# Taking the products of constants out of a decoder step's norm pauses, beginning and routing

## The chip, the cores and the metric

The kernel is one launch on one core of one Trainium2 chip. The metric is device time in microseconds, the median of the runs shown. The engines are named as in the profile: PE (TensorE; PEld is its weight load), DVE (VectorE), ACT (ScalarE), POOL (GpSimd), SP (SyncE, which here issues the weight DMAs).

## What is computed

Two layers of a decoder are run for 256 prompt tokens and 64 sample tokens (8 sequences of 8), 320 columns in all, model width 1024, all in fp32. Cut to what matters:

```
mod = (silu(c) @ w_ada[l] + b_ada[l])           # six vectors: sh1, sc1, g1, sh2, sc2, g2
h   = rmsnorm(x, norm_pre_mix[l]) * (1 + sc1) + sh1
mix = mixer(h)                                  # gMLP chunk gating and HGRN2, merged by w_out
x   = x + g1 * rmsnorm(mix, norm_post_mix[l])   # } a norm pause: post-norm, residual,
h   = rmsnorm(x, norm_pre_ffn[l]) * (1 + sc2) + sh2   # } pre-norm
f   = swiglu(h)        (layer 0: dense, 2816 wide)
f   = moe(h)           (layer 1: top 2 of 8 experts by h @ w_router, 2816 wide each)
x   = x + g2 * rmsnorm(f, norm_post_ffn[l])
```

No output depends on the products that this change is about: they multiply a tile of ones with a tile of constants into a PSUM bank, and nobody reads the result.

## The kernel before, in words

Activations lie with channels on the partitions: a tensor of 1024 channels is 8 tiles of 128 x 320. Every weight comes by DMA as fp32 (`raw`, 128 x 1024 a unit). ACT rounds it to fp32r (`whi`, L1844), DVE subtracts that from it (`wlo`, L808), and PE multiplies three times: `whi` with the high part of the activation (L2554), `whi` with its low part (L2555), `wlo` with the high part (L2600). In `channels` (from L2580) a unit's 16 high products come first and then its 8 low ones. The order of the work is written by hand, one stream of instructions for each engine; an engine executes its stream strictly in order, and semaphores tie the streams together.

**The beginning.** PE first multiplies ones with ones six times (L2645; this stays), then transposes the inputs, sums the squares, and multiplies the conditioning rows with `w_ada` unit by unit as the DMAs land (L2521). The second `turn` (L2538) gives the shift vectors; DVE and ACT then make the operand `h1h`/`h1l` tile by tile (L1953, L1957, L1020, L1023), and the first main product (L2554) waits for each channel tile by the semaphore `operand`.

**A norm pause** stands between two stages, three times: after the mixer's `w_out` of layer 0, after the dense block of layer 0 and after `w_out` of layer 1. In it

- `stat` (L2479): the squares of a tile (ACT, L1864) are summed over channels by products with ones, four column quarters side by side;
- `spread_rstd` (L2490): the reciprocal root (ACT L1876, DVE L865) is spread over the partitions, 8 recorded products;
- `pause(s, half)` (L2521): products of the conditioning rows with four units of `w_ada` each, kept back for the pause, 32 recorded products;
- DVE normalises and adds to `x` two tiles at a time (L969, L973); ACT squares the new `x` (L1864);
- after the second `spread_rstd` DVE and ACT make the next operand, channel tile by channel tile (L900 to L923 and L1917, L1924), and the first products of the next stage wait for them.

PE's stream of one pause is this (L2907 to L2915, and the same at L2950 to L2958):

```
spread_rstd(4); pause(2 * l, 0); stats(range(0, 2))
warm(2, 0)
stats(range(2, 4)); pause(2 * l, 1); stats(range(4, KD)); spread_rstd(3)
if l == 0:
    warm(3, 0)
```

**The routing** (L2969 to L3051) follows the third pause. PE multiplies `h` with the router's columns (L2978, 8 output columns a product, 48 recorded products in two groups of 24), between and after them it turns `h` into token rows (`hm`, L2966), which ACT and DVE copy and SP stores. DVE takes the two best experts and the softmax (ACT's `exp`, L2169), PE adds up positions (L2991, L2993), DVE makes the selection, PE picks the token numbers (L3020), and POOL gathers the rows of the first expert by an indirect DMA (L2446). Meanwhile PE turns the gates (L3042, 32 recorded products), ACT copies them (L2175), PE turns the gathered rows (`fill`, L3004), ACT copies those (L2160) and the experts' products begin (L3415). From then on SP streams 512 KB expert weight tiles into a ring to the end of the kernel.

**The products of constants.** `warm(n, bank)` (L2509) issues n products of `ONES` with 320 columns of the constants `CF`, in plain fp32, into a bank that the next stage starts anew. Each is recorded as two instructions. It waits for nothing and signals nothing. It is called at L2683 (3, the beginning), L2911 and L2917 (2 and 3, pause of layer 0's mixer; at L2911 also 2 in layer 1), L2953 and L2958 (2 and 3, the dense block's pause), and L2970, L2989, L2998 and L3045 (4, 1, 2 and 3, the routing): 25 products, 50 recorded instructions.

Of the kernel before, what the change touches and what calls it, by code (L numbers as in the profile page):

```python
# [35 lines left out]
T = TP + TS  # L36
# [347 lines left out]
def build(nc, a, out):  # L384
    ctx = ExitStack()
    with ctx:
        sems = {}

        def sem(name):
            if name not in sems:  # L390
                sems[name] = ctx.enter_context(nc.semaphore(name))
            return sems[name]
# [4 lines left out]
        def at(name, shape, dt, offset):  # L397
            return nc.alloc_sbuf_tensor_at(name, shape, dt, offset=low + offset, align_bytes=16)
# [117 lines left out]
        CF = at("cf", [P, C_N], F32, o)  # L516
# [6 lines left out]
        ONES = ONESR[:, :].bitcast(F32)  # L523
# [45 lines left out]
        PS = ctx.enter_context(nc.psum_tensor("ps", [P, 8, 512], F32))  # L569
# [1888 lines left out]
        def _(pe):  # L2458
            M = nc.tensor
# [24 lines left out]
            def spread_rstd(bank):  # L2484


                counts["spread"] += 1
                pe.wait_ge(sem("recip_made"), counts["spread"])
                for c in range(4):
                    ins = M.matmul(PS[:, bank, c * TQ:(c + 1) * TQ],  # L2490
                                   CF[:, C_ID + 32 * c:C_ID + 32 * c + 1].broadcast_to([P, P]), RSTD[:, 0:TQ],
                                   start=True, stop=True, skip_group_check=True)
                ins.then_inc(sem("rstd_spread"), 1)
# [12 lines left out]
                                   stop=(n >= 3), skip_group_check=True)  # L2506
                ins.then_inc(sq_used, 1)

            def warm(n, bank):  # L2509

                for _ in range(n):
                    M.matmul(PS[:, bank, 0:T], ONES[:, :], CF[:, 0:T], start=True, stop=True)

            def stats(tiles=range(KD)):
                for k in tiles:
                    stat(k == 0, k == KD - 1)
# [17 lines left out]
            def turn(g, src, bank):  # L2534

                pe.wait_ge(rows_out, g + 1)
                for t in range(2):
                    ins = M.transpose(PS[:, bank, CW + t * P:CW + (t + 1) * P], src[:, t * P:(t + 1) * P], ident)  # L2538
                ins.then_inc(turned, 1)
# [12 lines left out]
            def high_products(out_, w, v, start):  # L2552

                M.matmul(out_, w, v[0], start=start, stop=False, skip_group_check=True)  # L2554
                M.matmul(out_, w, v[1], start=False, stop=False, skip_group_check=True)  # L2555

            def lo_ready(c, part):
                pe.wait_ge(lo_made, BEFORE[PLACE[c, part]] + 1)

            def unit(c, part):  # L2560

                u = PLACE[c, part]
                pe.wait_ge(hi_made, BEFORE[u] + 1)
                if part == 0 and c >= 2:
                    pe.wait_ge(psum_out, c - 1)
                return WHI[:, BEFORE[u] % HI_UNITS, :], WLO[:, u % RAW_UNITS, :]
# [9 lines left out]
            def pause_turn(s):  # L2576

                turn(PAUSE_GROUPS[s], ROWSP, 7)

            def channels(parts, l, need=None, order=BY_M, side=None, middle=None, end=None):  # L2580


                def one(c, j, n):
                    for part in range(2):
                        if part and middle is not None:
                            middle()
                        w = unit(c, part)
                        for slot in range(8 * part, 8 * part + 8):
                            m, k = order[slot]
                            s = slice(k % 4 * CW + m * P, k % 4 * CW + (m + 1) * P)  # L2590
                            t = slice(k * T, (k + 1) * T)
                            if need is not None:
                                need(k)
                            high_products(PS[:, 2 * j + m, 0:T], w[0][:, s], (parts[0][:, t], parts[1][:, t]), k == 0)
                            if side is not None:
                                side(slot)
                        lo_ready(c, part)
                        for m, k in order[8 * part:8 * part + 8]:
                            s = slice(k % 4 * CW + m * P, k % 4 * CW + (m + 1) * P)
                            ins = M.matmul(PS[:, 2 * j + m, 0:T], w[1][:, s], parts[0][:, k * T:(k + 1) * T],  # L2600
                                           start=False, stop=(k == KD - 1), skip_group_check=True)
                        ins.then_inc(unit_used, 1)
                    if end is not None:
                        end()
                    modulation(c, 1)
                return one
# [73 lines left out]
            for k in range(1, KD):  # L2680
                rows_unit(KD + k, k, 3)
            turn(1, ROWS0[:, 1, :], 3)
            warm(3, 0)  # L2683

            n_operand = 0
            read_at = {}
            for l in range(DEPTH):
# [73 lines left out]
                for k in range(4):  # L2761
# [14 lines left out]
                    for m in range(2):  # L2776
                        n = 2 * k + m
# [17 lines left out]
                for k in range(4):  # L2795
# [15 lines left out]
                    if k in (1, 2):  # L2811
                        pe.wait_ge(aux_out, x[0])
                        for n in range(2):
                            b = aux()
                            for h in range(4):
                                s = slice((4 * n + h) * P, (4 * n + h + 1) * P)
                                ins = M.matmul(PS[:, b, h * P:(h + 1) * P], KTM[:, k - 1, s], IT[:, k - 1, s],
                                               start=True, stop=True)
# [89 lines left out]
                pe.wait_ge(psum_out, BASE[l, "O"] + 3)  # L2908
                pause(2 * l, 0)
                stats(range(0, 2))  # L2910
                warm(2, 0)  # L2911
                stats(range(2, 4))
                pause(2 * l, 1)
                stats(range(4, KD))
                spread_rstd(3)  # L2915
                if l == 0:
                    warm(3, 0)  # L2917
                if l == 0:
                    for i in range(11):
                        for j in range(2):  # L2920
                            need = None if i + j else lambda d: pe.wait_ge(operand, n_operand + d + 1)
                            channels(H1, l, need, BY_M if i + j else BY_K)(GU_BASE + 2 * i + j, j, None)
                            if i + j == 0:
                                pause_turn(0)
                    n_operand += KD
                    for k in range(4):
                        c = DOWN_BASE + k
                        for part in range(6):
                            w = unit(c, part)
                            if k and part == 2:  # L2930
                                stats(range(2 * k - 2, 2 * k))
                            kfs = range(4 * part, min(4 * part + 4, KF))
                            for kf in kfs:
                                if k == 0 and kf % 2 == 0:
                                    pe.wait_ge(sem("ffn_lo"), kf // 2 + 1)
                                for m in range(2):
                                    s = slice(kf % 4 * CW + m * P, kf % 4 * CW + (m + 1) * P)
                                    high_products(PS[:, 2 * (k % 2) + m, 0:T], w[0][:, s],
                                                  (PRH[:, kf, :], PRL[:, kf, :]), kf == 0)
                            lo_ready(c, part)  # L2940
                            for kf in kfs:
                                for m in range(2):
                                    s = slice(kf % 4 * CW + m * P, kf % 4 * CW + (m + 1) * P)
                                    ins = M.matmul(PS[:, 2 * (k % 2) + m, 0:T], w[1][:, s], PRH[:, kf, :],  # L2944
                                                   start=False, stop=(kf == KF - 1), skip_group_check=True)
                            ins.then_inc(unit_used, 1)
                            modulation(c, part)
                    stats(range(KD - 2, KD))
                    spread_rstd(4)
                    pe.wait_ge(psum_out, DOWN_BASE + 3)  # L2950
                    pause(1, 0)
                    stats(range(0, 2))
                    warm(2, 0)  # L2953
                    stats(range(2, 4))
                    pause(1, 1)
                    stats(range(4, KD))
                    spread_rstd(3)
                    warm(3, 0)  # L2958


            def hm(i, h):
# [5 lines left out]
                ins.then_inc(sem("hm_in"), 1)  # L2967

            pe.wait_ge(psum_out, CHUNKS)  # L2969
            warm(4, 2)  # L2970
            pe.wait_ge(aux_out, x[0])
            pe.wait_ge(sem("wr_in"), 48)
            for d in range(KD):
                pe.wait_ge(sem("hs_made"), mark["hs"] - 1 + d // 4)
                pe.wait_ge(sem("hp_made"), d + 1)
                for t in range(TT):
                    n = P if t < 2 else TS
                    ins = M.matmul(PS[0:n, 0, 8 * t:8 * t + 8], HT2[:, d, t * P:t * P + n], WR[:, d, :],  # L2978
                                   start=(d == 0 and t == 0), stop=(d == KD - 1), skip_group_check=True)
# [6 lines left out]
                    pe.wait_ge(sem("hm0_out"), 1)  # L2986
                hm(i, 1)
            pe.wait_ge(sem("hm1_out"), 2)
            warm(1, 3)  # L2989
            pe.wait_ge(sem("sel_made"), 1)  # L2990
            M.matmul(PS[:, 1, 0:24], CF[:, C_TRI:C_TRI + P], SEL[:, :, :], start=True, stop=False, skip_group_check=True)  # L2991
            for e in range(TT):
# [2 lines left out]
                               skip_group_check=True)  # L2995
            ins.then_inc(sem("pos_in"), 1)
            pause_turn(2)
            warm(2, 3)  # L2998

            def fill(k, rows=XG, banks=FILL_BANKS):  # L3000

# [37 lines left out]
            for g in range(2):  # L3039
                for d in range(KD):  # L3040
                    gate = GE[:, d, :] if g else AM[:, d, 0:1].broadcast_to([P, P])
                    ins = M.matmul(PS[0:(P, TS)[g], GT_BANKS[g][d // 4], d % 4 * P:(d % 4 + 1) * P], gate, ident,  # L3042
                                   start=True, stop=True, skip_group_check=True)
            ins.then_inc(sem("gt_in"), 1)
            warm(3, 4)  # L3045
            pe.wait_ge(xg_in, 16)
            for k in range(2):
                if k:
# [420 lines left out]
            for i, (t, h) in enumerate(LAST_TILES):  # L3469
                n, t0 = (P if t < 2 else TS), P * t  # L3470
# [4 lines left out]
            for i, (t, h) in enumerate(LAST_TILES):  # L3475
                n, t0 = (P if t < 2 else TS), P * t
# [34 lines left out]
```

## Time and profile before

| | before |
|---|---|
| median of 3 runs | 1946.75 us (1945.53 to 1949.64) |
| the profiled execution's own time | 1951.62 us |
| its span in the profile | 1949.5 us |
| mean granted TensorE clock | 0.990 |
| PE busy | 1882.5 us (97%) |
| DVE, ACT, POOL busy | 956.8, 741.7, 127.8 us |
| DMA | 488.57 MB, mean 251 GB/s |

The profile is of one execution. Its own time is 2.1 us above its span; the times in rows are from the span's start. A granted clock of 1.00 is 2.4 GHz, 0.50 is 1.2 GHz. A busy share says little of what bounds the kernel: a row's bracket tells how long the engine was idle before an instruction and which instruction ended that. The ends of matmuls are modelled, so where two follow each other, the difference of their starts is the surer number.

### The profile page before, as it was taken

What the parts mean: (1) busy time and instruction counts of PE and PEld (TensorE: products, weight loads), DVE (VectorE), ACT (ScalarE), POOL (GpSimd) and SP (SyncE); (2) the same over time, 40 slices, a digit from 0 to 9 for tenths busy, and PEclk for the clock granted to TensorE, in tenths of its full rate; (3) what the DMA queues carried; (4) which work ended last, traced back from release to release, by engine and by line L of the source; (5) the groups of instructions that cost most, each with busy time, mean ns of one, the idle gap of its engine ahead of it and who ended that gap; (6) DMA issues with size and microseconds to landing.
All of it is one profiled execution on the core that took longest, in us unless ns stands there. A gap on an engine that the chain in (4) does not pass through costs nothing.

```text
span 1949.5 us, 30517 instructions
## 1 busy us (share of the span) xinstructions
PE 1882.5 (97%) x12497; PEld 1463.7 (75%) x12497; DVE 956.8 (49%) x1317; ACT 741.7 (38%) x927; POOL 127.8 (7%) x170
## 2 busy tenths in 40 slices
PE   7999999998999999999999999999999999999997
PEld 4999999997999989999999985356556655455443
DVE  4467554555444445585545642255455544433333
ACT  4434333445334334343334432144444444333222
POOL 2200001400000003000014010000000000000000
PEclk9999999999999999999999998999999999999999
DMA  9635356683665635533566748999999999899986
GB/s 358 210 124 160 115 167 181 195 273 87 197 212 181 233 119 174 156 115 96 162 193 206 238 160 308 403 387 381 400 397 387 380 409 384 299 324 354 352 309 241
DMA packets 276001, 488.57 MB, mean 251 GB/s; under 512 B 16951, under 2 KB 169641, under 8 KB 275858
## 3 DMA queue, kind: packets, MB, share of 16 engines
q1 hardware_dynamic: 266368, 458.02, 67.9%
q0 software_dynamic: 9472, 28.51, 4.7%
q8 instruction: 101, 1.65, 0.4%
q14 instruction: 42, 0.34, 0.1%
q10 hardware_dynamic: 18, 0.04, 0.0%
HBM read 473.91 MB, written 12.59 MB: 250 GB/s over the span
## 4 chain that ended last, share of the span: by engine, by line
PE 79%; DMA 9%; DVE 5%; SPq 3%; ACT 2%; issue 2%; POOL 1%; DVEq 0%; ACTq 0%; POOLq 0%
PE ps L2554 12%; PE ps L2555 11%; PE ps L2600 10%; PE ps L3263 6%; DMA mraw<-in_w_exp_up 3%; PE ps L3272 3%; PE ps L2624 3%; PE ps L3192 2%; PE ps L2633 2%; PE ps L3415 2%; DMA mraw<-in_w_exp_down 2%; SPq L738 2%; PE ps L3308 2%; PE ps L2521 2%; PE ps L3222 2%
## 5 line engine op out<-in xcount | busy, mean ns | idle before, releaser
L808 DVE TENSOR_TENSOR wlo<-raw,whi 128x1024 fp32r<-128x1024 f32 x244 | 289.1, 1212 | 309.6 <-ACT whi L1844 308.6
L2554 PE MATMUL ps<-h1h,whi 128*128 128x320 f32 x1248 | 386.1, 322 | 6.5 <-DVE h1l L915 3.9
L2555 PE MATMUL ps<-h1l,whi 128*128 128x320 f32 x1248 | 371.1, 310 | 0.0
L1844 ACT ACTIVATE whi<-raw 128x1024 fp32r<-128x1024 f32 x244 | 248.0, 1046 | 121.9 <-PE ps L2944 44.8
L2554 PEld LDWEIGHTS ps<-h1h,whi 128*128 128x128 f32 x1248 | 235.6, 189 | 22.8 <-issue 16.9
L1415 DVE TENSOR_TENSOR mhi<-mraw,mhi 128x2048 fp32r<-128x2048 f32 (+1 forms) x70 | 151.9, 2171 | 172.6 <-ACT mhi L2139 169.5
L2555 PEld LDWEIGHTS ps<-h1l,whi 128*128 128x128 f32 x1248 | 235.9, 189 | 0.2 <-issue 0.2
L2600 PE MATMUL ps<-h1h,wlo 128*128 128x320 f32 x1248 | 209.4, 310 | 0.0
L2139 ACT ACTIVATE mhi<-mraw 128x2048 fp32r<-128x2048 f32 (+1 forms) x70 | 127.0, 1814 | 206.6 <-DMA mraw<-in_w_exp_up 138.5
L2600 PEld LDWEIGHTS ps<-h1h,wlo 128*128 128x128 f32 x1248 | 189.0, 188 | 0.8 <-issue 0.8
L1649 DVE TENSOR_TENSOR mhi<-mraw,mhi 128x2048 fp32r<-128x2048 f32 (+1 forms) x35 | 75.9, 2169 | 120.2 <-PE ps L3314 115.0
L3192 PE MATMUL ps<-mraw,xef 128*64 128x512 f32 (+1 forms) x384 | 86.1, 569 | 0.0
L3263 PE MATMUL ps<-mraw,xefn 128*64 128x512 f32 (+1 forms) x384 | 83.9, 566 | 0.4 <-DVE y L1640 0.4
L3201 PE MATMUL ps<-mhi,xeh 128*128 128x512 f32 (+1 forms) x192 | 77.6, 404 | 4.3 <-ACT mhi L2139 4.1
L2554 PE MATMUL ps<-h2h,whi 128*128 128x320 f32 x256 | 77.0, 315 | 0.0
L2555 PE MATMUL ps<-h2l,whi 128*128 128x320 f32 x256 | 75.5, 309 | 0.0
L3202 PE MATMUL ps<-mhi,xel 128*128 128x512 f32 (+1 forms) x192 | 72.5, 378 | 0.0
L2147 ACT ACTIVATE mhi<-mraw 128x2048 fp32r<-128x2048 f32 (+1 forms) x35 | 63.3, 1809 | 22.6 <-DMA mraw<-in_w_exp_up 19.9
L3201 PEld LDWEIGHTS ps<-mhi,xeh 128*128 128x128 f32 x192 | 36.2, 189 | 44.8 <-ACT mhi L2139 32.9
L2624 PE MATMUL ps<-whi,h1h 128*128 128x256 f32 x256 | 63.9, 287 | 0.0
L2624 PE MATMUL ps<-whi,h1l 128*128 128x256 f32 x256 | 62.7, 283 | 0.0
L3208 PE MATMUL ps<-mhi,xeh 128*128 128x512 f32 (+1 forms) x192 | 51.8, 391 | 2.5 <-DVE mhi L1415 1.7
(513 smaller groups left out, 3020.7 us busy)
## 6 DMA issues: line engine op xcount, KB each, us to landing
mraw<-in_w_exp_down SPq DMA_DIRECT2D x176, 512.0 KB, 11.0
raw<-in_w_in SPq DMA_DIRECT2D x128, 512.0 KB, 3.9
mraw<-in_w_exp_gate SPq DMA_DIRECT2D x123, 512.0 KB, 9.8
mraw<-in_w_exp_up SPq DMA_DIRECT2D x123, 512.0 KB, 11.3
raw<-in_w_ada SPq DMA_DIRECT2D x64, 512.0 KB, 3.9
mraw<-in_w_exp_gate SPq DMA_DIRECT2D x59, 384.0 KB, 7.7
mraw<-in_w_exp_up SPq DMA_DIRECT2D x59, 384.0 KB, 9.6
pause<-in_w_ada SPq DMA_DIRECT2D x32, 512.0 KB, 6.9
```

The lines of the kernel that those rows point to most:

```text
L808: V.tensor_tensor(WLO[:, u % RAW_UNITS, 0:w], RAW[:, u % RAW_UNITS, 0:w], WHI[:, h % HI_UNITS, 0:w].bitcast(F32), ALU.subtract).then_inc(l ...
L1415: V.tensor_tensor(MHI[:, BOTH_HI + n % BOTH_LO, 0:w], MRAW[:, both.pair(n) % RAW_RING, 0:w], MHI[:, n % BOTH_HI, 0:w].bitcast(F32), ALU.su ...
L1649: V.tensor_tensor(MHI[:, THREE_LO_SLOT, 0:w], MRAW[:, triple_pair(WIDE_AT[n]) % RAW_RING, 0:w], MHI[:, n % THREE_HI, 0:w].bitcast(F32), AL ...
L1844: A.activation(WHI[:, h % HI_UNITS, 0:w], RAW[:, u % RAW_UNITS, 0:w], ACT.Copy).then_inc(hi_made, 1)
L2139: A.activation(MHI[:, n % BOTH_HI, 0:w], MRAW[:, pair % RAW_RING, 0:w], ACT.Copy).then_inc(m_hi, 1)
L2554: M.matmul(out_, w, v[0], start=start, stop=False, skip_group_check=True)
L2555: M.matmul(out_, w, v[1], start=False, stop=False, skip_group_check=True)
L2600: ins = M.matmul(PS[:, 2 * j + m, 0:T], w[1][:, s], parts[0][:, k * T:(k + 1) * T], start=False, stop=(k == KD - 1), skip_group_check=True)
L2624: M.matmul(place(t), x_[:, q], w[0][:, s], start=(k == 0 and t != 1 and x_ is parts[0]), stop=False, skip_group_check=True)
L3192: ins = M.matmul(PS[HALF * j:HALF * j + HALF, half_, 0:w], XEF2[:, k, :], raw_[:, (2 * j + n) * w:(2 * j + n + 1) * w], start=(k == 0), st ...
L3201: M.matmul(PS[:, bank, 0:w], XEH[:, k, :], hi_[:, s], start=(k == 0), stop=False)
L3263: ins = M.matmul(PS[HALF * j:HALF * j + HALF, out_, 0:w], tokens_[:, k, :], raw_[:, (2 * j + n) * w:(2 * j + n + 1) * w], start=(k == 0), ...
```

## The change

The helper and all its calls go. Nothing is put in their place, and nothing else is moved.

```diff
-            def warm(n, bank):
-
-                for _ in range(n):
-                    M.matmul(PS[:, bank, 0:T], ONES[:, :], CF[:, 0:T], start=True, stop=True)
-
...
             turn(1, ROWS0[:, 1, :], 3)
-            warm(3, 0)
...
                 stats(range(0, 2))
-                warm(2, 0)
                 stats(range(2, 4))
                 pause(2 * l, 1)
                 stats(range(4, KD))
                 spread_rstd(3)
-                if l == 0:
-                    warm(3, 0)
...
                     stats(range(0, 2))
-                    warm(2, 0)
                     stats(range(2, 4))
                     pause(1, 1)
                     stats(range(4, KD))
                     spread_rstd(3)
-                    warm(3, 0)
...
             pe.wait_ge(psum_out, CHUNKS)
-            warm(4, 2)
             pe.wait_ge(aux_out, x[0])
...
             pe.wait_ge(sem("hm1_out"), 2)
-            warm(1, 3)
             pe.wait_ge(sem("sel_made"), 1)
...
             pause_turn(2)
-            warm(2, 3)
...
             ins.then_inc(sem("gt_in"), 1)
-            warm(3, 4)
             pe.wait_ge(xg_in, 16)
```

## Rows read from the trace of the kernel before

**Rows 1.** The page, part 4: the chain that ended last, share of the span by engine

```profile
PE 79%; DMA 9%; DVE 5%; SPq 3%; ACT 2%; issue 2%; POOL 1%; DVEq 0%; ACTq 0%; POOLq 0%
```

**Rows 2.** The instructions of L2512: ns min/median/max, first and last start us

```profile
L2512 PE MATMUL ps<-cf,ones x50: 432/432/741, 32.6 to 1191.7; 128*128 128x320 f32 x50
```

**Rows 3.** The timeline of the beginning: start us, us, engine line, [idle before, releaser]

```profile
32.57 3.41 PE L2512 MATMUL ps<-cf,ones 128*128 128x320 f32 x6
...
33.96 0.29 DVE L1020 TENSOR_TENSOR h1l<-ht,h1h 128x128 fp32r<-128x128 f32 x1 [0.45 <-ACT h1h L1953]
...
43.46 0.41 PE L2554 MATMUL ps<-h1h,whi 128*128 128x320 f32 x1 [0.61 <-DVE h1l L1023]
...
44.73 1.33 PE L2600 MATMUL ps<-h1h,wlo 128*128 128x320 f32 x8
```

**Rows 4.** The timeline of the first norm pause, 453 to 475 us

```profile
461.44 1.34 PE L2512 MATMUL ps<-cf,ones 128*128 128x320 f32 x4
...
461.74 0.83 ACT L1864 ACTIVATE t<-x 128x320 f32<-128x320 f32 x2 [0.64 <-DVE x L973]
...
462.71 0.48 PE L2479 MATMUL ps<-t,ones 128*32 128x80 f32 x16
463.01 1.91 PE L2521 MATMUL ps<-pause,csf 128*9 128x256 f32 x32
463.54 1.57 ACT L1864 ACTIVATE t<-x 128x320 f32<-128x320 f32 x4 [0.96 <-DVE x L973]
...
464.74 0.76 PE L2479 MATMUL ps<-t,ones 128*32 128x80 f32 x32
...
467.66 1.82 PE L2512 MATMUL ps<-cf,ones 128*128 128x320 f32 x6
...
470.58 0.39 PE L2554 MATMUL ps<-h1h,whi 128*128 128x320 f32 x1 [1.10 <-DVE h1l L915]
...
473.77 0.42 PE L2554 MATMUL ps<-h1h,whi 128*128 128x320 f32 x1 [0.85 <-DVE h1l L915]
```

**Rows 5.** Stretches: us, busy (x) of PE, PEld, DVE, ACT, POOL, clock, DMA

```profile
454.40:470.58 16.18, 11.03 (x171) 6.85 (x171) 12.21 (x21) 8.86 (x20) 0.00 (x0) 1.00 0.12 33
...
1145.29:1148.71 3.42, 1.70 (x24) 1.08 (x22) 0.65 (x1) 1.90 (x6) 2.14 (x4) 1.00 0.14 10
...
1162.36:1165.77 3.41, 3.41 (x28) 3.00 (x27) 3.17 (x8) 2.64 (x8) 0.00 (x0) 1.00 1.03 417
1165.77:1172.60 6.83, 6.83 (x34) 6.61 (x32) 2.10 (x4) 0.40 (x1) 0.00 (x0) 0.50 1.03 410
...
1182.84:1189.67 6.83, 6.15 (x28) 5.96 (x29) 5.15 (x27) 0.00 (x0) 1.04 (x1) 0.50 0.40 89
```

**Rows 6.** The timeline where PE ran at a clock of 0.50, wholly or in part

```profile
886.35 0.47 PE L2554 MATMUL ps<-h1h,whi 128*128 128x320 f32 x1
886.62 0.47 PE L2555 MATMUL ps<-h1l,whi 128*128 128x320 f32 x1
...
1150.54 2.67 PE L2521 MATMUL ps<-pause,csf 128*9 128x256 f32 x32
```

**Rows 7.** The timeline of the routing, 1160 to 1194 us

```profile
1160.35 2.36 PE L2512 MATMUL ps<-cf,ones 128*128 128x320 f32 x8
...
1162.63 3.05 PE L2978 MATMUL ps<-wr,ht 128*128 128x8 f32 x24
...
1168.07 4.97 PE L2978 MATMUL ps<-wr,ht 128*128 128x8 f32 x24
...
1177.48 1.24 PE L2512 MATMUL ps<-cf,ones 128*128 128x320 f32 x4
1177.96 0.21 ACT L2169 ACTIVATE pr<-pr 128x3 f32<-128x3 f32 x1
...
1190.45 2.04 ACT L2175 ACTIVATE gt<-ps 128x512 f32<-128x512 f32 x4 [12.28 <-PE ps L3042]
...
1192.00 1.04 PE L3004 MATMUL ps<-cf,xg 128*128 128x128 f32 x8
```

## The prediction

> **What bounds the kernel now.** I read the chain that ended last first: PE holds 79% of it [rows 1], so PE's order of work decides, and a product that nobody reads could cost its full length. Next come the removed instructions: 50 records, median 432 ns each, the longest 741 ns [rows 2]. The spread says that some ran at another clock. In the pause their group starts at 461.44 and the next product at 462.71, 1.27 us for four records; in the beginning six records took 3.41 us [rows 3, 4]. Taken flat (4 records to 1.1 us at the full clock, 6 to 3.3 us at half), the 50 records are some 15 us of PE time, 0.8% of the kernel. Whether any of it is on the path is read from what the product behind each group waited for. Last, the clock: stretches without dense PE work are followed by a granted clock of 0.50, and what comes then runs at half speed [rows 5, 6].
>
> No change under about 0.2% (3.9 us) can be told from none for this kernel; the three runs shown lie 4.1 us apart.
>
> **What the removal gives directly**, group by group.
>
> *Beginning, 3 products.* They hold PE from 32.57 to 35.98, while the first low part of the operand is ready at 33.96 + 0.29 = 34.25 [rows 3]. The first main products could start some 1.1 us earlier. But the later channel tiles come from DVE: at 43.46 PE has been idle 0.61 us again for the last ones [rows 3]. All that PE gains before is lost there: 0. The bounds: -0.6 us if DVE too moved up by as much as PE idles there, +1.3 us if the half clock, which ended here at 35.96, lasted past 43.46 and up to 46 (half of 2.5 us).
>
> *The short groups in the three pauses, 2 products each.* The square of the third tile is ready only about 462.2 and that of the fourth at 461.74 + 0.83 = 462.57; the sums of both start at 462.71 [rows 4]. Without the group the fourth sum still can't start before 462.6, so the row products at 463.01 come about 0.2 us earlier. Behind them the last four squares end at 463.54 + 1.57 = 465.11, while the sums began at 464.74 and end at 465.50 [rows 4]: the last sum waits for its square, ACT sets the end, and ACT's squares wait for DVE. Direct gain 0; at most 0.2 us each.
>
> *The long groups, 3 products, in the two pauses of layer 0.* After them PE idles 1.10 us until DVE's `h1l` [rows 4]. Direct gain 0, and nothing less or more, since DVE waits for nothing of theirs.
>
> *Routing, 4 products.* Eight records from 1160.35 at the full clock (4 to 1.1 us) end near 1162.5, and the router products begin at 1162.63 [rows 7], so at most 2.3 us could be won; but they need DVE's and ACT's new tiles, which in the pauses of layer 0 came 2.9 us after the spread (467.66 to 470.58) [rows 4]. 0, bounds 0 and 0.5. *1 and 2 products:* the second group starts at 1177.48, ACT's exponential is at 1177.96 and DVE's selection hangs on that [rows 7]; the position sums ahead have slack. 0. *3 products before the gathered rows are turned:* the turns start at 1192.00 where they could at 1190.4. But ACT copies the gates until 1190.45 + 2.04 = 1192.49 and only then the turned rows, of which the first four turns (half of 1.04 us) are ready at 1192.5 [rows 7]. Gain 0.15 us, bounds 0 and 1.6.
>
> So the direct sum is -0.15 us out of 15 us of work: the cover is DVE's and ACT's work in every place. Were the cover gone, it would be the -4 us of the second rival.
>
> **What the removal takes away: the clock.** The first pause ran at 1.00 all through, with 11.03 us of PE work in 16.18, of which 3.2 us are constants [rows 4, 5]. A stretch as thin as what would be left is in the trace too: 1145.29 to 1148.71, PE busy 1.70 of 3.42 us with 80-column sums and drains among it, and the next stretch runs at 0.50 (its row products took 2.67 us instead of 1.91) [rows 4 to 6]. The routing shows the same: the router products, 8 columns each, count as busy (3.41 of 3.41 us) and still the clock falls at 1165.77 [rows 5]. Its price there is plain: 24 router products took 3.05 us at the full clock and 4.97 us at half [rows 7].
>
> *Routing.* Before the router products PE has only the 8 spread products and the 4 constants. Without the constants the thin stretch begins 2.1 us earlier or more, so the fall comes before the first group of 24 and not after it. That group is in PE's chain, one tile after the other, so +4.97 - 3.05 = **+1.9 us**; bounds 0 (the fall comes no earlier) and 3 us (more of the turns behind it at half).
>
> *End of each pause of layer 0.* After the sums end (465.5) and up to 470.58 PE would have only the spread products, 1.1 us in 5.1, thinner than the stretch that brought 0.50 at 1148.71 [rows 4, 5]. I take a fall there as certain, somewhere about 470.58. At half, main products start 0.267 us apart [rows 6]; at full, eight take 1.33 us with the last one's drain of some 0.3 in it, so 0.147 [rows 3]. Three channel tiles of four products must be done before the fourth tile arrives at 473.77: 12 x 0.267 = 3.2 us from 470.58 ends at 473.8. So the half clock is free up to there, PE having idled 0.85 us, and each further microsecond costs 0.45. The half stretches in the trace last 3.4 or 6.8 us [rows 5]: between 0 and 1.2 us (up to 476.4). I take 0.7 each, **+1.4 us**.
>
> *Middle of each of the three pauses.* Between the first row products and 462.7 PE would have 0.55 us of sums only. If the clock falls there, the second row products, the sums behind them and with them the whole chain run at half: 32 row products are 1.7 us of starts at full and twice that at half, so +1.7 less the 0.2 of slack won, 1.5 us. This stretch is about as thin as the one of 1145.29 but shorter, so the fall will come at some and not at others; I take 4 in 10, 3 x 0.4 x 1.5 = **+1.8 us**, bounds 0 and 4.5.
>
> *After the fall in the routing* the gates' turns run at half already, 6.83 us on the chain's stretch to 1189.67 [rows 5]; nothing changes there.
>
> **The sum:** -0.15 + 1.9 + 1.4 + 1.8 = +4.95, say +5 us. The routing carries it to the end, since experts' products begin behind it. Against the profiled execution that is 1951.62 + 5 = 1956.6; it lay 4.9 us above the median, so the median goes from 1946.75 to about **1951.8 us**.
>
> The Trainium skill, "TensorE: Matmul & The Clock Gate", under "Why this matters for your kernels", asks that PE not stand wholly idle between bursts, and names a gap longer than any that the norm pauses would have. By it they would keep their clock, and the sum would be the first rival's. The routing goes against it: there the clock fell after a stretch in which PE had work all the time [rows 5].
>
> **The rivals.**
>
> *The pauses keep their clock* (not slower). Sums, spreads and row products are enough, as they were in every stretch of the layer 0 pauses before; only the routing's +1.9 - 0.15 is left or, if the fall there comes no earlier, nothing. 1946.6 to 1948.5 us, no change that can be told. For it: the pause at 454 held 1.00 although it has idle time of over 1 us twice [rows 4]. Against it: the fall at 1148.71. What decides is whether the granted clock in 462 to 476 stays 1.00. Chance 0.25.
>
> *The constants stood in the way* (faster). PE is 79% of the chain [rows 1]; if the products that follow were released earlier than the rows let me see, the beginning gives 0.6 us, each short group 0.2, and the group before the gathered rows 1.6 instead of 0.15, with some of 1.1 us at the positions: about -4 us, 1943 us. It decides if the first expert product starts earlier, counted from the third pause. Against it is each wait named above. Chance 0.07.
>
> *The clock stays down for long* (slower by more). Each middle falls (4.5), each end costs 1.2 (2.4), the beginning 1.3, the routing 3: +11 us, 1958 us. It decides if the half clock lasts past 476 in the pauses. Chance 0.10.
>
> **How the numbers follow.** The forecast has 0.58. Its own range is +2.5 to +8, by the pauses' chance to fall or not; with its median, four fifths of it lie above 3.9 us: 0.46. With the last rival, slower by over 0.2% has 0.56, and some of the first rival's runs drift there: 0.58. The second rival and the scatter of three runs give faster 0.08. The rest, 0.34, is within 0.2%. The range leaves out the second rival and half of the third: 1945.8 to 1956.5 us.
>
> **What the changed profile would show.** No L2512. Right: the granted clock at 0.50 before or during the first 24 router products, which then take near 5 us; a stretch of 0.50 about the first main products after each pause of layer 0, with their starts 0.27 us apart; in some pauses row products of over 3 us. The last square sum still right behind its square, the first `h1l` no earlier after the spread. Wrong: the pauses at 1.00 throughout (first rival), or the experts beginning sooner after the third pause than before (second rival).

## The result and the profile after

| | before | after |
|---|---|---|
| median of 6 runs | 1948.41 us (1945.53 to 1952.23) | 1959.39 us |
| the profiled execution | 1951.62 us | 1959.40 us |
| its span | 1949.5 us | 1957.3 us |
| mean granted clock | 0.990 | 0.982 |

The ratio is 1.0045, interval 1.0030 to 1.0061: slower by 5.8 to 11.9 us of 1948. One execution of the changed kernel took 5969.86 us; it is left out of the ratio, and the other five lie at 1953.96 to 1960.16. Measured again beside 28 runs of the kernel before, the change gave 1.0033 (1.0020 to 1.0045), +6.4 us. The forecast had +5 us, and 1959.39 is above its range. Two readings of the same runs have to be kept apart: the two medians of the table lie 11.0 us apart, the ratio makes it 8.8; and the forecast's range was laid on the 1946.75 us of three runs, where six gave 1948.41.

First the stretches at a clock of 0.50 behind the beginning, as in [rows 5] (us, busy of PE, PEld, DVE, ACT, POOL, clock, DMA):

```profile
461.62:465.03 3.41, 3.40 (x44) 1.48 (x44) 2.60 (x5) 1.58 (x5) 0.00 (x0) 0.50 0.02 5
...
471.86:475.27 3.41, 3.32 (x12) 2.92 (x13) 3.34 (x10) 1.79 (x4) 0.00 (x0) 0.50 0.00 0
721.03:724.45 3.42, 3.42 (x30) 1.79 (x33) 2.29 (x4) 0.62 (x1) 0.00 (x0) 0.50 0.01 4
734.69:738.10 3.41, 3.32 (x12) 3.30 (x13) 3.34 (x9) 2.04 (x5) 0.00 (x0) 0.50 0.00 0
1154.53:1157.94 3.41, 3.41 (x44) 1.48 (x39) 2.34 (x4) 1.57 (x4) 1.85 (x1) 0.50 1.02 407
1161.35:1171.59 10.24, 8.51 (x41) 8.21 (x42) 6.61 (x16) 3.41 (x8) 0.00 (x0) 0.50 1.03 409
...
1175.01:1188.66 13.65, 9.07 (x41) 8.02 (x40) 9.83 (x64) 3.17 (x6) 1.04 (x1) 0.50 0.43 134
1663.11:1666.53 3.42, 3.42 (x10) 0.99 (x6) 0.42 (x1) 1.87 (x2) 0.00 (x0) 0.50 0.54 191
1939.59:1946.42 6.83, 5.31 (x22) 3.86 (x22) 2.07 (x3) 2.72 (x8) 0.00 (x0) 0.50 0.01 2
```

Every pause lost its clock, twice each in layer 0, and the routing, up to 1188.66, had it at 1.00 only from 1171.59 to 1175.01. The last two rows are in no pause: one is among the experts' products, the other in the last stage of the kernel. In the beginning the clock was 0.50 from 28.13 to 41.78 us, before from 29.14 to 35.96.

The first pause, as in [rows 4] (timeline of PE, with one row of ACT; L2516 is the L2521 of before, L2549 the L2554):

```profile
455.87 1.12 PE L2490 MATMUL ps<-rstd,cf 128*128 128x80 f32 x8 [1.20 <-DVE rstd L865]
...
459.95 0.61 PE L2479 MATMUL ps<-t,ones 128*32 128x80 f32 x16 [1.12 <-ACT t L1864]
461.33 0.85 PE L2479 MATMUL ps<-t,ones 128*32 128x80 f32 x16 [0.76 <-ACT t L1864]
461.96 3.43 PE L2516 MATMUL ps<-pause,csf 128*9 128x256 f32 x32
462.60 1.56 ACT L1864 ACTIVATE t<-x 128x320 f32<-128x320 f32 x4 [0.96 <-DVE x L973]
465.21 0.73 PE L2479 MATMUL ps<-t,ones 128*32 128x80 f32 x32
467.15 1.12 PE L2490 MATMUL ps<-rstd,cf 128*128 128x80 f32 x8 [1.21 <-DVE rstd L865]
471.02 0.39 PE L2549 MATMUL ps<-h1h,whi 128*128 128x320 f32 x1 [2.76 <-DVE h1l L915]
```

The 32 row products took 3.43 us, not 1.91, and now PE sets the end of the sums: the squares are done at 464.16, and the last sums start at 465.21. Before, the last sum waited for its square. The first main product waits 2.76 us for DVE where it waited 1.10: the long group had filled only idle time.

The routing, as in [rows 7] (L2966 is the L2978 of before, L3028 the L3042):

```profile
1163.09 5.11 PE L2966 MATMUL ps<-wr,ht 128*128 128x8 f32 x24 [2.12 <-ACT ht L1921]
1168.12 2.77 PE L2955 MATMUL ps<-cf,ht 128*64 128x128 f32 x12
1170.68 3.37 PE L2966 MATMUL ps<-wr,ht 128*128 128x8 f32 x24
```

The router products wait for ACT, so the four constants had hidden there too, and their first group takes 5.11 us instead of 3.05. The second takes less than before, 3.37 against 4.97, since in the profiled execution of before the clock had fallen in between.

And the last stage, behind the last expert products (L3272, after L3257), first of before, then of after (timeline of PE):

```profile
1930.86 1.94 PE L3272 MATMUL ps<-mraw,gtfn 128*64 128x512 f32 x8
1934.99 1.09 PE L3463 MATMUL ps<-cf,sa 128*128 128x128 f32 x8 [2.19 <-issue]
1935.83 0.49 PE L3471 MATMUL ps<-yeh,pts 128*128 128x512 f32 x1
1936.16 0.60 PE L3463 MATMUL ps<-cf,sa 128*128 128x128 f32 x4
```

```profile
1934.47 1.94 PE L3257 MATMUL ps<-mraw,gtfn 128*64 128x512 f32 x8
1938.52 1.09 PE L3448 MATMUL ps<-cf,sa 128*128 128x128 f32 x8 [2.12 <-issue]
1939.43 0.68 PE L3456 MATMUL ps<-yeh,pts 128*128 128x512 f32 x1
1939.91 0.41 PE L3448 MATMUL ps<-cf,sa 128*128 128x128 f32 x1
1941.84 0.90 PE L3448 MATMUL ps<-cf,sa 128*128 128x128 f32 x3 [1.52 <-issue]
1942.39 0.78 PE L3456 MATMUL ps<-yeh,pts 128*128 128x512 f32 x1
1942.97 1.05 PE L3448 MATMUL ps<-cf,sa 128*128 128x128 f32 x4
```

In the middle of four transposes PE idles 1.52 us and nothing that the profile shows held it (`issue`), and what follows runs at the half clock. From the first transpose to the end of the span before took 1949.5 - 1935.0 = 14.5 us, after 1957.3 - 1938.5 = 18.8; this is the "last stage" below. The change touches nothing there. But it takes 50 matmuls and their weight loads, 100 instructions, out of the stream ahead of it (the page counts 30517 before and 30418 after, one record being missing), and just before the gap one packet of the instruction queue moves (the DMA view of after, 1939.3 to 1942.3 us):

```profile
GB/s 0 0 0 218 0 0 0 0 0 0 0 0 0 0 0 0 0 0 0 0 0 0 0 0 0 0 0 0 0 0 0 0 0 0 0 0 0 0 0 0
DMA packets 1, 0.02 MB, mean 5 GB/s; under 512 B 0, under 2 KB 0, under 8 KB 0
## 3 DMA queue, kind: packets, MB, share of 16 engines
q8 instruction: 1, 0.02, 1.9%
```

The packet moves in the fourth of 40 slices, at about 1939.55; PE falls idle at 1940.3. Such a packet alone is no sign of a gap: before has one too, half a microsecond after its transposes began, and no gap behind it (the same view of before, 1934.5 to 1937.5 us, the 13th slice):

```profile
GB/s 0 0 0 0 0 0 0 0 0 0 0 0 218 0 0 0 0 0 0 0 0 0 0 0 0 0 0 0 0 0 0 0 0 0 0 0 0 0 0 0
```

Taken stage by stage, the two profiled executions differ by 7.8 us: +0.5 up to the first router product, -1.0 in the routing (29.9 us for 30.9), +4.1 from the first expert product to the last stage (745.5 for 741.4) and +4.3 in the last stage. One pair of profiles is thus a poor bill of the change: nothing was removed among the experts' products, and the routing came out shorter.

### The profile page after: what moved, and what is told of

Same layout as the page of the kernel before. It is cut to its first block, busy times and chain, and to the rows that moved or that the text cites. A ratio compares the mean times of both kernels' runs of the same rounds, so it can differ in the third digit from the quotient of the medians.

```text
span 1957.3 us, 30418 instructions
## 1 busy us (share of the span) xinstructions
PE 1881.1 (96%) x12447; PEld 1461.6 (75%) x12447; DVE 957.0 (49%) x1317; ACT 741.9 (38%) x927; POOL 128.2 (7%) x170
## 4 chain that ended last, share of the span: by engine, by line
PE 78%; DMA 8%; DVE 5%; SPq 4%; ACT 2%; issue 2%; POOL 1%; DVEq 0%; ACTq 0%; POOLq 0%
PE ps L2549 12%; PE ps L2550 12%; PE ps L2595 10%; PE ps L3248 6%; SPq L738 3%; DMA mraw<-in_w_exp_up 3%; PE ps L2619 3%; DMA mraw<-in_w_exp_down 3%; PE ps L3257 3%; PE ps L2628 2%; PE ps L3400 2%; PE ps L3177 2%; PE ps L3293 2%; PE ps L2516 2%; PE ps L3207 2%
## 5 line engine op out<-in xcount | busy, mean ns | idle before, releaser
L2549 PE MATMUL ps<-h1h,whi 128*128 128x320 f32 x1248 | 387.4, 323 | 8.8 <-DVE h1l L915 5.5
L2549 PEld LDWEIGHTS ps<-h1h,whi 128*128 128x128 f32 x1248 | 237.1, 190 | 23.6 <-issue 21.1
L2549 PE MATMUL ps<-h2h,whi 128*128 128x320 f32 x256 | 77.0, 315 | 0.0
## 6 DMA issues: line engine op xcount, KB each, us to landing
mraw<-in_w_exp_up SPq DMA_DIRECT2D x123, 512.0 KB, 11.3
```

## The experiments

Two theories: the loss is the **clock** that the constants held, or part of it is their place in the **instruction stream**. All were timed in five rounds beside the kernel before. After each time stand two stretches of its one profiled execution: the routing, from the first router product to the first expert product (before 1162.63 to 1193.56, 30.9 us), and the last stage as above (14.5 us).

**The change again, `all_out`.**

> The change itself once more, as the measure for the three kernels beside it. Clock theory: +6 to +11 us over before, with a granted clock of 0.50 at the end of both layer 0 pauses and from before the first 24 router products. Instruction stream theory (the removed products were also instructions, and without them every later instruction lies elsewhere in the stream that is fetched in blocks): the last stage shows again the 1.52 us in which TensorE sits idle before a transpose of sa with nothing to wait for, at the same instruction, and some 4 us of the whole loss lie behind the last expert product.

1956.73 us, 1.0033 (1.0020 to 1.0045). Routing 33.0 us, last stage 18.4, with the gap:

```profile
1942.62 0.90 PE L3448 MATMUL ps<-cf,sa 128*128 128x128 f32 x3 [0.96 <-issue]
```

**All 25 kept, but short, `short_all`.** In effect (the column count is a parameter in the kernel that ran):

```diff
-    M.matmul(PS[:, bank, 0:T], ONES[:, :], CF[:, 0:T], start=True, stop=True)
+    M.matmul(PS[:, bank, 0:2], ONES[:, :], CF[:, 0:2], start=True, stop=True)
```

> All 25 products stay, but with 2 columns instead of 320: the same number of instructions and no more than 0.1 us of work each. Clock theory: as the change, +6 to +11 us. Instruction stream theory: the 1.52 us gap in the last stage is gone and so is the half clock that it feeds there; only +3 to +6 us are left. If neither holds and the products' own time had been on the path, it is faster than before.

1953.21 us, 1.0016 (1.0007 to 1.0026), +3.1 us: half of the +6.4 beside it. Routing 33.1 us, last stage 14.9, and a single wait of `issue` there:

```profile
1936.74 1.09 PE L3463 MATMUL ps<-cf,sa 128*128 128x128 f32 x8 [1.78 <-issue]
```

So about 3 us of the change's loss need fewer instructions, not less work. The two intervals overlap (+1.4 to +5.1 us here, +3.9 to +8.8 for `all_out`), but both contain the scatter of before; the kernels' own runs, 11 and 6 of the same rounds, have means 3.7 us apart, 1.6 to 5.6 if the runs are drawn anew, which is clear of the noise.

**The change, padded, `out_pad25`.** After each of seven units of the beginning:

```diff
+                for _ in range([4, 4, 4, 4, 3, 3, 3][k - 1]):
+                    M.matmul(PS[0:2, 0, 0:2], ONES[:, 0:2], CF[:, 0:2], start=True, stop=True)
```

> The change, with 25 products of 2 columns by 2 put into the DMA waits of the beginning (after L2521), so that from the first layer on every instruction lies where it did before. Instruction stream theory: the gap of 1.3 us or more before a transpose of sa late in the last stage is gone; last stage from its first transpose of sa to the end near 14.5 us, not 18.4; +2 to +4.5 us over before, as the kernel with 25 short products. Clock theory alone: as the change, +5.5 to +8 us.

1954.17 us, 1.0026 (1.0013 to 1.0038), +5.1 us. The second gap is gone; routing 29.3 us, last stage 16.1 us. The time lies between what the two theories gave and its interval reaches both, so the traces decide here, not the time.

**Before, with the stream moved, `before_pad39` and `before_pad64`.** The same padding in the kernel before, 39 and 64 products (156 and 256 instructions).

> The kernel before with all its products of constants, and 39 products of 2 columns by 2 more in the DMA waits of the beginning: 156 instructions more, which is the change's 100 fewer if the stream is fetched in blocks of 256 (1.65 MB in 101 packets by the page, 64 bytes an instruction). Instruction stream theory: the gap in the last stage appears though nothing of the constants is gone, and the time is +2 to +4 us over before. Clock theory alone: within 1 us of before.

> The kernel before and 64 products of 2 columns by 2 in the DMA waits of the beginning, 256 instructions, one whole block of the stream. Instruction stream theory: the second gap of the last stage is not there (one wait of issue before the transposes of sa, 14.4 to 16.1 us from the first of them to the end), within 1.5 us of before. If the 39 short products themselves made the gap, by their number, it is there again.

With 39: 1950.41 us, 1.0008 (0.9998 to 1.0018), routing 26.1, last stage **18.4** us. With 64: 1948.02 us, 0.9999 (0.9989 to 1.0009), routing 27.4, last stage 16.9, above the 14.4 to 16.1 expected, with a stretch of 0.50 from 1930.25 to 1933.66 in it. The gap appears with 39 in a kernel that has all its constants, at the same transpose as after the change:

```profile
1928.38 1.25 PE L3465 MATMUL ps<-cf,sa 128*128 128x128 f32 x8 [1.95 <-issue]
1929.46 0.79 PE L3473 MATMUL ps<-yeh,pts 128*128 128x512 f32 x1
1930.05 0.41 PE L3465 MATMUL ps<-cf,sa 128*128 128x128 f32 x1
1931.51 0.80 PE L3465 MATMUL ps<-cf,sa 128*128 128x128 f32 x3 [1.05 <-issue]
```

and with 64 it does not:

```profile
1928.07 1.09 PE L3465 MATMUL ps<-cf,sa 128*128 128x128 f32 x8 [1.37 <-issue]
```

That shows the gap's cause to be the place in the stream and not the number of padding products, as far as one profiled execution of each kernel can. Its price in time is less sure: with 39 the whole kernel was only 1.6 us slower (-0.4 to +3.5), below the +2 to +4 expected.

**One place at a time, at the same instruction count.** The call gets 2 columns at the lines named: `short_pauses` (L2911, L2917, L2953, L2958), `short_routing` (L2970, L2989, L2998, L3045), `short_r4` (L2970), `short_later3` (L2989, L2998, L3045).

> Only the products in the norm pauses (L2911, L2917, L2953, L2958) are cut to 2 columns. Clock theory: +3 to +5 us (two ends at 0.7 to 1.7, three middles at 0 to 1.5 each), with 0.50 in 462 to 476 and 725 to 739. Theory that only the routing needs its clock: 0 to +1.

> Only the products in the routing (L2970, L2989, L2998, L3045) are cut to 2 columns. Clock theory as predicted: +1.7 us or a little more, the first 24 router products near 5 us. Theory that the half clock only comes earlier and also rises earlier, so that what is lost in the first group of router products is won back in the turns and the second group: -1 to +0.5 us.

> Only the 4 products ahead of the router products (L2970) are cut to 2 columns. Theory that this group alone makes the routing's cost: +2 to +3.5 us, as with all four groups cut, and 0.50 from before the first router product in the profile. Theory that the products later in the routing bring the clock back for the gates' turns: 0 to +1 us.

> Only the three later groups of the routing (L2989, L2998, L3045) are cut to 2 columns. Theory that the 4 products ahead of the router products carry the routing alone: within 1 us of before. Theory that each group shares in it: +1 to +2 us.

| | median | ratio (interval) | routing | last stage |
|---|---|---|---|---|
| short_pauses | 1948.81 | 0.9997 (0.9987 to 1.0006) | 26.5 | 15.3 |
| short_routing | 1952.46 | 1.0012 (1.0003 to 1.0022) | 33.1 | 14.5 |
| short_r4 | 1952.47 | 1.0019 (1.0007 to 1.0031) | 30.7 | 14.7 |
| short_later3 | 1949.65 | 0.9998 (0.9989 to 1.0007) | 28.6 | 15.0 |

In the timing the pauses cost nothing that can be told (expected +3 to +5 by the clock theory), though their clock did fall, in `short_pauses` as well (its stretches):

```profile
457.09:460.51 3.42, 3.42 (x48) 1.51 (x40) 3.42 (x5) 1.52 (x3) 0.00 (x0) 0.50 0.00 0
467.33:474.16 6.83, 4.68 (x18) 4.63 (x18) 6.72 (x18) 3.88 (x8) 0.00 (x0) 0.50 0.00 0
1156.83:1177.31 20.48, 16.21 (x134) 13.66 (x126) 13.33 (x63) 7.06 (x15) 0.62 (x2) 1.00 0.94 368
```

The last row holds the first half of the routing, with the clock at 1.00 up to 1177.31; the gates' turns behind it ran at 0.50. The two groups of router products and what follows:

```profile
1161.73 3.06 PE L2978 MATMUL ps<-wr,ht 128*128 128x8 f32 x24
1164.72 1.50 PE L2966 MATMUL ps<-cf,ht 128*64 128x128 f32 x12
1166.05 2.98 PE L2978 MATMUL ps<-wr,ht 128*128 128x8 f32 x24
```

and the same three in `short_routing`, all at half:

```profile
1162.86 5.11 PE L2978 MATMUL ps<-wr,ht 128*128 128x8 f32 x24 [1.29 <-ACT ht L1921]
1167.90 2.77 PE L2966 MATMUL ps<-cf,ht 128*64 128x128 f32 x12
1170.46 4.97 PE L2978 MATMUL ps<-wr,ht 128*128 128x8 f32 x24
```

12.6 us against 7.3 up to the end of the second group. The four products of L2970 carry this: cutting them alone costs 3.7 us (1.4 to 6.0), cutting the three later groups nothing that can be told (-2.1 to +1.4).

**The change with only those four kept, `out_but_r4`** (and 21 short products as padding).

> The change, but the 4 products ahead of the router products stay, and 21 products of 2 columns by 2 at the beginning keep every later instruction where it was before. If the routing's clock and the place in the stream are the whole loss: within 1.5 us of before, routing from its first product to the first expert product 26 to 31 us instead of 29 to 33, last stage 14.4 to 16.1 us. If the pauses cost what was predicted (+3.2 us): +2 to +4.

1951.00 us, 1.0008 (0.9996 to 1.0019): +1.6 us, within -0.8 to +3.7. Routing 29.2 us, last stage 14.8. This agrees with the routing and the place being most of the loss. Its interval also reaches the +2 to +4 that the pauses would cost as predicted, so it does not rule them out.

**More constants, `fill_routing` and `hold_routing`.** The first has the last two pieces of this diff, the second all of it.

```diff
                 if d == 3:
                     for i in range(TT):
                         hm(i, 0)
+                    warm(1, 2)
+                if d == 5:
+                    warm(1, 2)
...
-            warm(2, 3)
+            warm(4, 3)
...
             pick(PS[:, 0, 0:2]).then_inc(sem("pick_in"), 1)
+            warm(1, 3)
```

> The kernel before with 2 more products of constants at L2998 and 1 after the pick at L3020, all in time in which TensorE idles for DVE. If the clock is held by them, the gates' turns (L3042) take 3.5 us instead of 6.8: -2 to -3.5 us under before. If they only stand in the way or the clock falls all the same: 0 to +1 us.

> The kernel before with 5 more products of constants: 1 after the first group of router products, 1 in the second, 2 more at L2998 and 1 after the pick. The two in the groups cost 2.2 us on the path. If the clock is then held through the routing in nearly every execution, the routing takes 26 to 27 us always, where before it took 26 to 31 by luck: -0.5 to -2.5 us. If it falls all the same: +1 to +2 us.

`fill_routing`: 1949.65 us, 1.0001 (0.9990 to 1.0012). Its gates' turns did run at the full clock in the profiled execution:

```profile
1180.44 2.02 PE L3043 MATMUL ps<-cf,am 128*128 128x128 f32 x16 [0.77 <-DVE am L939]
1182.39 1.96 PE L3043 MATMUL ps<-cf,ge 128*64 128x128 f32 x16
```

3.9 us for 6.8, routing 26.8, yet no time was won over 12 runs (1.0001, where -2 to -3.5 us had been expected); whether most of them kept that clock, a profile of one can't tell. `hold_routing`: 1949.76 us, 1.0007 (0.9998 to 1.0017), routing 30.6: the clock fell all the same at 1161.92 and again at 1168.74, in spite of the two products at 1164.68 and 1166.95. No version was faster than the kernel before, clear of the noise.

## Why the prediction was wrong

**Right: the direct gain is next to nil.** The waits behind the removed groups grew instead: 1.10 to 2.76 us in the pause, and 2.12 us where the router products had followed the four at once. Only the group ahead of the gathered rows had stood in the way: from the end of the gates' turns to the first expert product 3.2 us passed before and 2.8 after, 0.4 us less where 0.15 was summed. In the beginning the five kernels without its three full products came to 1.00 at 39.0 to 41.8 us, eight of the nine others at 33.8 to 37.2; the first pause began at 455.5 to 456.4 in the former and at 454.2 to 456.8 in the latter, so that cost nothing to be seen, as predicted. No kernel with fewer or shorter constants was faster, clear of the noise. The rival in which they stood in the way is out.

**Right: the clock falls about where it was said.** In all six profiled executions without full constants in the pauses it fell at the end of both layer 0 pauses, and in the middle in 6 pauses of 18 (4 in 10 was said); in the eight with them it never began to fall at either place. The first router group took 5.11 us where 4.97 was foretold. The price of a middle was right as well: in the first pause the two spreads lie 467.15 - 455.87 = 11.3 us apart, where it was 9.9 before, 1.4 us for the 1.5 of the sum. The second pause lost its clock at 721.03, ahead of where its constants had stood; four of the eight executions with all the pauses' constants (`before_pad39`, `before_pad64`, `fill_routing`, `hold_routing`) did the same at the start of both layer 0 pauses. Those falls are not the constants' doing, and that these pauses hold 1.00 throughout had been read from one execution.

**Too high: the pauses, +3.2 us.** Two ends at 0.7 and three middles at 0.6 were summed. An end cost 0 to 0.9 us in the first pause: from its first main product to the next pause 249.0 to 249.9 us passed in the six executions, 249.0 to 249.1 in the eight. From the first spread of the first pause to the first router product the six took 706.0 to 707.4 us, 706.6 in the mean, the eight 703.5 to 706.6, 704.8 in the mean: 1.8 us. The timing of `short_pauses`, -0.6 us (-2.5 to +1.2), shows less. So the size is somewhere from nothing to 2 us. The prediction also read the half stretches as 3.4 or 6.8 us long; that from 1165.77 lasted 10.24 us (the row in [rows 5] stops at 1172.60). Those at the ends of the pauses lasted 3.4 or 6.8.

**Perhaps too low: the routing, +1.75 us.** It took only the first group as lost, because in the profiled execution of before the second ran at half anyway [rows 5, 7]. That was one of several courses: with the four products kept, the routing took 26.1 to 30.9 us in eight profiled executions, 28.3 in the mean, with them gone or short 29.2 to 33.1 in six, 31.5 in the mean. The timed effect is +2.3 us (0.6 to 4.3) with all four groups cut and +3.7 (1.4 to 6.0) with L2970 alone; both intervals hold 1.75.

**The step that failed: the sum had no term for the place in the instruction stream.** It took the removed products as work and as clock, not as instructions. The place shows behind the last expert product: a gap of 0.96 to 1.52 us and a last stage of 18.4 to 18.8 us in all three profiled executions with the stream so placed (after, `all_out`, `before_pad39`), against 14.5 to 16.9 us and no such gap in the eleven others. Counted from the end of the last expert product, the three take 20.3 to 20.8 us, eight others 16.6 to 16.9, and 18.3 to 18.4 the remaining three (`out_pad25`, `before_pad64`, `fill_routing`), in which a stretch of 0.50 of 3.4 us fell there without the gap. With the gap that stretch lasts 6.8 us, and it begins ahead of the gap, so the gap does not start it; that it prolongs it is likely, not shown. In time the place has three prices: `all_out` less `short_all` 6.4 - 3.1 = 3.3 us, `all_out` less `out_pad25` 6.4 - 5.1 = 1.3 us, `before_pad39` 1.6 us. Only the first, timed in the same rounds, is clear of the noise; the three differ by 2 us, and why stays open.

The time left the range for two reasons. The 1946.75 us under it was 1.7 us low; on 1948.41 it would have ended at 1958.2. The other 1.2 us is less than any of the three prices of the missing term. That +5 lies near the measured +6.4 to +8.8 is partly luck: in the profiled executions the two clock terms came to 1.8 and 3.2 us, where 3.2 and 1.75 had been summed, so their errors cancel, and the missing term adds to them.

Two things stay open. Why the first measurement gave 2.4 us more than the second; the intervals overlap. And the experts' products: from the first of them to the last stage the fourteen executions took 740.6 to 745.5 us, and the three longest (after, `out_pad25`, `out_but_r4`) are those with a stretch of 0.50 at about 1661 to 1667. `all_out`, the same kernel as after, had none there and took 743.0, so whether the change has a part in it the runs do not tell.

The Trainium skill, "TensorE: Matmul & The Clock Gate", "Why this matters for your kernels", had been set against the routing: by its rule PE must stand idle, and longer than it did in the pauses, for the clock to fall. The trace after goes against it a second time: 461.62 to 465.03 ran at 0.50 although the longest wait of PE ahead of it in that pause was 1.20 us.

## What to carry to other kernels

Work that nobody reads can still be worth its place when it runs only in another engine's shadow: read first what the instruction behind it waits for, then what clock the stretch after it needs. One profile is one course of the clock; where a thin stretch leads into dense work, look at several executions before a term is billed at its price, and compare stage by stage, since stages that nothing was changed in differ too. And an edit that changes the number of instructions should be timed beside one that does the same with the number kept.

## What the runs showed that was not expected

A transposing loop was broken by 1.0 to 1.5 us of `issue` when 100 instructions had gone, or 156 had come, ahead of it, and not with 256 more; in after, the gap begins less than a microsecond after a 16 KB packet (0.02 MB by the view) of the instruction queue. Router products with 8 columns kept PE busy while its clock stood at 0.50 (8.51 of 10.24 us in 1161.35 to 1171.59); in `short_pauses`, with the four constants ahead of them, the same products ran at 1.00. And one unchanged piece of the kernel, the routing, took 26.1, 26.5, 27.4 and 30.9 us in one profiled execution each of `before_pad39`, `short_pauses`, `before_pad64` and before.
